# Split-weight buffers of a one-core fp32r kernel placed 64 bytes further along, from 128 to 192 modulo 256 bytes

## The kernel before

| operand | before | after |
|---|---|---|
| raw buffers `weights0` to `weights3` | 128 | 128 |
| `weights_hi`, `weights_lo`, every block (blocks are 512 bytes, buffers 2048) | 128 | 192 |
| the two further `weights_hi` and `weights_lo` in the arena | 64 | 64 |
| activations of 256 columns: `xn_hi`, `xn_lo`, and all split activations in the arena (rows of 1024 bytes) | 64 | 64 |
| activations of 272 columns: `xn_hi`, `xn_lo`, `mlp_hi`, `mlp_lo` (rows of 1280 bytes) | 192 | 192 |
| split activations of `ab_out` and `c_out` (rows of 1088 bytes, one row per k) | 64, 128, 192, 0 in turn | the same |

## Time and profile before

### The profile page before, as it was taken

How to read it: one execution, slowest core, us unless ns; L and a number is a source line. 1 busy time by engine, 2 the same in 40 slices (tenths; PEclk the granted TensorE clock), 3 DMA queues, 4 the chain that set the end, 5 groups by cost and what they waited for, 6 DMA issues and landing times.

```text
span 2596.3 us, 54007 instructions
## 1 busy us (share of the span) xinstructions
PE 2457.7 (95%) x18747; PEld 2341.4 (90%) x18747; DVE 1758.2 (68%) x3497; ACT 1348.3 (52%) x2827; POOL 10.3 (0%) x17
## 2 busy tenths in 40 slices
PE   7999998979999999999999999998998999988998
PEld 7899998979989999899988999988877999877998
DVE  6566666977657677776575576656776775777764
ACT  4555556556554444465555565555663444454443
POOL 0000000000000000000000000000000000000000
PEclk9999999999999999899999999999998999998999
DMA  6535563225644333356645356643433555322553
GB/s 203 175 122 170 184 197 117 93 89 171 203 144 130 124 126 121 104 165 185 202 131 181 124 168 192 205 152 121 130 106 98 169 175 174 122 97 90 171 177 129
DMA packets 103383, 385.43 MB, mean 148 GB/s; under 512 B 11344, under 2 KB 13392, under 8 KB 103024
## 3 DMA queue, kind: packets, MB, share of 16 engines
q1 hardware_dynamic: 102784, 381.90, 46.0%
q0 software_dynamic: 496, 2.24, 0.2%
HBM read 383.05 MB, written 1.05 MB: 148 GB/s over the span
## 4 chain that ended last, share of the span: by engine, by line
PE 85%; DVE 9%; ACT 3%; issue 2%; DMA 0%; DVEq 0%; ACTq 0%; SPq 0%
PE acc L488 24%; PE acc L489 23%; PE acc L490 23%; PE acc L667 2%; DVE weights_lo L1628 2%; PE acc L651 1%; PE acc L653 1%; PE acc L652 1%; PE acc L531 1%; PE acc L746 1%; PE acc L705 1%; ACT weights_hi L1062 1%; PE acc L592 1%; PE acc L835 1%; PE acc L726 1%
## 5 line engine op out<-in xcount | busy, mean ns | idle before, releaser
L1628 DVE TENSOR_TENSOR weights_lo<-weights,weights_hi 128x512 fp32r<-128x512 f32 (+1 forms) x1392 | 905.1, 683 | 445.9 <-ACT weights_hi L1062 441.1
L488 PE MATMUL acc<-xn_parts,weights_hi 128*128 128x256 f32 (+1 forms) x3456 | 996.3, 288 | 41.4 <-DVE xn_parts L1742 14.1
L489 PE MATMUL acc<-xn_parts,weights_hi 128*128 128x256 f32 (+1 forms) x3456 | 980.3, 284 | 0.0
L490 PE MATMUL acc<-xn_parts,weights_lo 128*128 128x256 f32 (+1 forms) x3456 | 980.0, 284 | 0.0
L1062 ACT ACTIVATE weights_hi<-weights 128x512 fp32r<-128x512 f32 (+1 forms) x1392 | 811.1, 620 | 250.5 <-PE acc L490 220.6
L488 PEld LDWEIGHTS acc<-xn_parts,weights_hi 128*128 128x128 f32 x3456 | 658.3, 190 | 59.9 <-issue 46.2
L489 PEld LDWEIGHTS acc<-xn_parts,weights_hi 128*128 128x128 f32 x3456 | 657.6, 190 | 1.0
L490 PEld LDWEIGHTS acc<-xn_parts,weights_lo 128*128 128x128 f32 x3456 | 658.5, 191 | 0.0
L488 PE MATMUL acc<-arena_r,weights_hi 128*128 128x256 f32 (+1 forms) x1792 | 511.6, 285 | 9.8 <-DVE arena_r L2090 4.9
L489 PE MATMUL acc<-arena_r,weights_hi 128*128 128x256 f32 (+1 forms) x1792 | 507.3, 283 | 0.0
L490 PE MATMUL acc<-arena_r,weights_lo 128*128 128x256 f32 (+1 forms) x1792 | 507.3, 283 | 0.0
(11 more groups left out here) (286 smaller groups left out, 2494.0 us busy)
## 6 DMA issues: line engine op xcount, KB each, us to landing
weights<-in_ffn_in SPq DMA_DIRECT2D x176, 512.0 KB, 3.6
weights<-in_ffn_out SPq DMA_DIRECT2D x64, 704.0 KB, 4.1
weights<-in_att_in SPq DMA_DIRECT2D x72, 512.0 KB, 3.5
weights<-in_mlp_in SPq DMA_DIRECT2D x64, 512.0 KB, 3.4
weights<-in_mlp_out SPq DMA_DIRECT2D x64, 512.0 KB, 3.5
weights<-in_ret_qk SPq DMA_DIRECT2D x32, 512.0 KB, 3.5
weights<-in_ret_v SPq DMA_DIRECT2D x32, 512.0 KB, 3.8
weights<-in_ret_g SPq DMA_DIRECT2D x32, 512.0 KB, 3.5
```

The lines of the kernel that those rows point to most:

```text
L488: nc.tensor.matmul(acc, hi, src_hi, start=first, stop=False)
L489: nc.tensor.matmul(acc, hi, src_lo, start=False, stop=False)
L490: return nc.tensor.matmul(acc, lo, src_hi, start=False, stop=last)
L1628: nc.vector.tensor_tensor(w_lo[sub % phase.subs][:, 0:n, :], raw[slot][:, j * SUB:j * SUB + n, :], w_hi[sub % phase.subs][:, 0:n, :].bitca ...
```

## The change

Sixteen float32 columns (64 bytes) of padding are allocated ahead of the `weights_hi` buffers, and forty-eight (192 bytes) behind the `weights_lo` buffers. All that is allocated after these moves by 256 bytes in all, the arena not at all. No instruction is added, removed or put in another order; the operand addresses alone differ.

```diff
         raw = [sb(f"weights{s}", [P, SLOT_TILES, P]) for s in range(SLOTS)]
+        sb("weights_offset", [P, 16])
         w_hi = [sbr(f"weights_hi{s}", [P, SUB, P]) for s in range(SUBS)]
         w_lo = [sbr(f"weights_lo{s}", [P, SUB, P]) for s in range(SUBS)]
+        sb("input_offset", [P, 48])
         h = sb("h", [P, DC, S2])
```

## The result

The changed kernel takes 2623.70 us in the median of 5 runs (2622.76 to 2625.97); the kernel before, in 5 runs beside it, 2597.39 (2596.29 to 2609.27). The ratio is 1.0094, with a 95% interval of 1.0072 to 1.0117: slower by 26 us between the medians, and by 25 between the profiled executions. The forecast was 2645, 47 us more. So the sign is right, the size is a little over half, and the time lies inside the stated range of 2595 to 2656, though outside the forecast's own of 2639 to 2652.

A forecast was written before the change was run, and what follows sets the result against it. TensorE's pace was taken as the bound. 256-column matmuls gave 42.8 + 9.2 = 52.0 us, less 1 and 3, say 47; all else 0; 2598.1 + 47 = 2645 us. Own range 2639 to 2652, stated range 2595 to 2656.

The forecast's parts named there:

- The bound and the place of the cost: Whole kernel: TensorE's pace sets the time, the split costs nothing more, 256-column matmuls pay, 52.0 us before deductions.
- Their d goes from -64 to -128: 256-column matmuls, 10560: streaming less stationary address, modulo 256 bytes, goes from -64 to -128, the same as +128.
- nothing happens: Rival, 12%: the address isn't the cause, fast or slow is drawn anew each run; 2598 us.
- I take 120.0: 256-column matmuls: new pace 120.0 ns, from 113.3 in fast stages and 117.8 in slow ones; together 52.0 us more.
- half-clock stretches: 256-column matmuls at half clock or starting after a wait hide part of the cost: 2%, 1 us off.
- waits: conv_in and att_in: part of the longer matmuls vanishes into waits on VectorE and ScalarE, 3 us of 6.8 hidden.
- one reading covers all five: Priced values of d: -64 is the one favourable relation, each other costs 13.3 ns over the ideal.
- to the digit: `ab_out`, 272 columns: three relations at 13.3 ns and -64 at 11.1 average 12.8 over the ideal, matching the trace.
- 272 columns: no change: 5184 matmuls of 272 columns: 13.3 ns over the ideal before and after, no change; bounds 31 us either way.
- ret_values: 384 matmuls of 512 columns, d from +64 to +128: taken as 0, a step either way being 2.6 us.
- The draw: 256-column stages at d = -64: two paces, 113.3 and 117.8 ns; a stage keeps the one it falls into.
- slow pace everywhere: Rival, 10%: 256-column stages at 113.3 ns go to 117.8, the others stay; 28 us more, 2626.

The follow-up runs named there:

- inputs_back_64: Against the changed kernel: weights back at 128, all activations and the arena 64 bytes back, same relations; 2624.28 us, ratio to before 1.0133.
- all_back_64: Against the kernel before: every SBUF buffer, arena included, 64 bytes further back, relations kept; 2590.25 us against 2589.54, ratio 0.9996.
- pace: Separate kernel, TensorE alone: stationary and streaming buffers at four places each, 256, 272 and 512 columns; at 256, 120.0 ns at d = 0, 113.3 or 117.8 at -64.
- lo_only: Against the changed kernel: weights_hi back at 128, weights_lo stays at 192; 2625.21 us, ratio to before 1.0147.
- wide_zero: Against the kernel before: only the 272-column activations moved, from 192 to 128, making their d 0; 2584.91 us, ratio 0.9983.
- weights_at_64: Against the changed kernel: split weights at 64 by other pad widths, d = 0 at 256 columns, +128 at 272; 2639.55 us, ratio to before 1.0180.
- weights_at_0: Against the changed kernel: split weights at 0 by other pad widths, d = +64 at 256 columns, -64 at 272; 2607.67 us, ratio to before 1.0054.
- draws: Separate kernel, TensorE alone: d = -64 groups behind one to eight other matmuls, then mixed triples; 5.62 or 5.82 us per group, mixed triples 118.2 ns.

## Why the prediction was right in sign and too high

**The bound and the place of the cost: right.** TensorE's pace sets the time, the split keeps 689 and 624 ns, and the cost falls on 256 columns, most on the stages that had been fast.

**"Their d goes from -64 to -128": right, and shown.** `inputs_back_64` gets after's time with the weights at their old place, `all_back_64` gets before's with everything moved, and `pace` gives the step with TensorE alone. What in TensorE or the memory makes it is not shown. The rival "nothing happens" is out.

**"I take 120.0": the term that was mis-sized.** After runs at 118.76 ns over 10,185 distances at full clock, before at 115.13 over 10,169. (120.0 - 118.76) x 10,169 = 12.6 us too much in a gross sum of 52. The measured gross is (118.76 - 115.13) x 10,169 = 36.9; the stages grew by 32.0, so 4.9 us less came through. The prediction gave such a rest to half-clock stretches (1 us) and waits (3 us); these runs show the rest, not its parts.

The value came from "one reading covers all five", that every relation but -64 costs 13.3 ns over the ideal. It had a row at d = 0 with 256 columns and one at d = +128 with 272, and carried the excess from the one width to the other. `pace` shows that each width has its own order: d = 0 is the worst place at 256 columns, the second best at 272, and the best at 512. An excess over the ideal is no constant of the relation. That the earlier trace rows fitted the mean "to the digit" was no proof: `lo_only` shows that loads of unlike relations don't average, and by the table of `pace` the mean of the four at 272 columns would be 125.5, not the 126.1 that `ab_out` has.

**"272 columns: no change": wrong by 4.4 us.** At d = 0 they take 125.3 ns, not the 126.7 of d = +64; `wide_zero` shows the same 4 us alone. `ret_values` cost 1.2 us where 0 was taken, within its stated 2.6. About 4 us between the stages went the good way, 3.0 of them because the granted clock did not fall behind `att_in`. The prediction had no term for it. `inputs_back_64`, with after's relations, and `weights_at_64` kept that clock as well, and `lo_only`, at 118.2 ns, did not; whether the change or luck did it, no run decides.

Together: 52.0 - 12.6 is 39.4, where the distances give 36.9 (they are fewer than the 10,560 matmuls, with a few more slow ones than the prediction's list of stages). From there 36.9 - 4.9 - 4.4 + 1.2 - 3.7 = 25.1.

**The draw.** The prediction read two paces at one set of addresses and took the draw of the traced execution as given. That was the right base for a sum against this execution, but the result then depends on it: beside before's 2589.54 us on the chip of `inputs_back_64` the same relations cost 1.3%, or 35 us, not 0.9%. The rival "slow pace everywhere", 2626, comes nearest to the number, and its mechanism is wrong: the pace is 118.7, not 117.8, and in `weights_at_0`, where 117.8 does hold in nearly all of them, the 256-column stages are 20.0 us longer than before's in the two traces, not 32.0.

**The Trainium skill.** `pace` has one active engine and its distance between matmuls moves from 113.3 to 120.0 ns with the address alone. The rule of "SBUF — State Buffer", section "SBUF: two separate sides", that TensorE's port never waits on another engine, is left standing by this. "TensorE: Matmul & The Clock Gate", section "Step-by-step: what each phase is for", gives TensorE two independent read ports; were that all, the place of one operand against the other should not count, and in these runs it does. The same page, section "Wait — 56ns, not 53.3ns?", gives N/2.4 ns and about 2.5 more between matmuls, 109.2 ns at 256 columns. No run here with a weight load per matmul was under 113.3, and none was made without the loads.

## What to carry to other kernels

Where every fp32r matmul loads its own stationary block and TensorE is the bound, the address of the streaming operand less that of the stationary one, modulo 256 bytes, was worth up to 6% of the pace here (113.3 against 120.0 ns). Measure all four relations at each width with TensorE alone (one kernel of 0.6 ms did it here), then allocate so that all operands of a matmul stream have the good one, since one buffer of three out of step spoiled the other two (`lo_only`). One group per relation isn't enough: `pace` showed both paces at -64 and missed the fast one of +64. Don't carry an excess from one width to another, and take the time of before from several executions when a stage can sit at two paces.

## What the runs showed of the hardware that was not expected

- The best relation changes with the width: -64 at 256 and 272 columns (113.3, 123.3 ns), 0 at 512 (226.7), where -64 is the worst (233.3).
- With 256 columns a relation can have two paces: 113.3 or 117.8 ns at -64 and, in one stage of `weights_at_0`, at +64; 118.7 or 120.0 at +128. A pace was kept through nearly the whole of stages of 1056 matmuls, and at -64 the number of matmuls just ahead was enough to change it (`draws`).
- With one load of three at +128 and two at -64 a matmul takes 118.25 ns (mean of the three); with all three 118.7, with none 113.3.
- Steps of 64 bytes were tried alone; what smaller ones do, and what in the memory or in TensorE makes the pattern, stays open.
